# Half-size products for ten units of a convolution's input and 21 of the last FFN, with the weight sums on VectorE and on GpSimd

## The reference, cut to what matters

```python
def short_conv_mixer(h, w_in, conv_w, w_out):          # first mixer of the first block
    b_gate, c_gate, u = jnp.split(h @ w_in, 3, axis=-1)
    v = c_gate * u
    conv = ...                                          # causal, 3 taps per channel
    return (b_gate * conv) @ w_out

def conv_ffn(h, w_up, conv_w, conv_b, w_down, grid):    # last FFN of the second block
    gate, up = jnp.split(h @ w_up, 2, axis=-1)
    gate = dwconv_grid(gate, conv_w, conv_b, grid)      # 3x3 taps per channel, grid 4 x 64
    return (jax.nn.gelu(gate, approximate=True) * up) @ w_down
```

## Time and profile before

| what | value |
|---|---|
| median of 3 runs | 3435.51 us (3429.36 to 3435.82) |
| the profiled execution | 3436.1 us |
| its span, first to last instruction | 3434.3 us |
| instructions in the span | 54420 |
| PE busy | 3189.5 us, 93% of the span |
| DVE busy | 995.1 us, 29% |
| ACT busy | 593.8 us, 17% |
| POOL busy | 225.3 us, 7% |
| mean granted clock of TensorE | 0.943 of 2.4 GHz |

### The profile page before, as it was taken

One profiled execution on the slowest core, in us unless ns is written; L12 is line 12 of the kernel. 1 busy time (PEld: TensorE's weight loads), 2 busy tenths in 40 slices (PEclk: granted clock), 3 DMA queues, 4 the chain that ended last, 5 costly groups with the idle time before them and its releaser, 6 DMA issues. The chain is left out here.

```text
span 3434.3 us, 54420 instructions
## 1 busy us (share of the span) xinstructions
PE 3189.5 (93%) x24210; PEld 1926.6 (56%) x24210; DVE 995.1 (29%) x2185; ACT 593.8 (17%) x1336; POOL 225.3 (7%) x198
## 2 busy tenths in 40 slices
PE   7999996899999999989988999999898888888998
PEld 4788784633323332254765544444544777777887
DVE  0255115311100110023064233420313555461560
ACT  1010012210000000032144200000202343432100
POOL 0000000000000000000032100000000223131000
PEclk9999998899999999979989899999798989998999
DMA  9778841169988889922002133333211000004340
GB/s 365 280 281 326 326 176 65 56 265 377 377 352 344 341 360 376 390 77 74 2 1 98 49 123 146 119 127 121 80 50 58 14 21 17 14 3 180 120 155 13
DMA packets 88492, 577.04 MB, mean 168 GB/s; under 512 B 9536, under 2 KB 15936, under 8 KB 20672
## 3 DMA queue, kind: packets, MB, share of 16 engines
q1 hardware_dynamic: 84800, 568.27, 42.4%
q10 hardware_dynamic: 3456, 5.24, 0.4%
HBM read 567.19 MB, written 6.29 MB: 167 GB/s over the span
## 5 line engine op out<-in xcount | busy, mean ns | idle before, releaser
L267 PE MATMUL ps<-H,ring 128*128 128x256 f32 (+1 forms) x2928 | 909.4, 473 | 19.3 <-ACT H L557 8.9
L267 PEld LDWEIGHTS ps<-H,ring 128*128 128x128 f32 x2928 | 567.4, 195 | 361.1 <-issue 309.5
L267 PE MATMUL ps<-W,ring 128*128 128x256 f32 (+1 forms) x1488 | 470.3, 477 | 11.3 <-DVE W L2858 8.0
L1706 PE MATMUL ps<-ring,W 128*32 128x512 f32 (+1 forms) x2816 | 474.1, 596 | 1.7 <-ACT H L1766 1.7
L267 PEld LDWEIGHTS ps<-W,ring 128*128 128x128 f32 x1488 | 284.6, 193 | 199.2 <-issue 172.3
L1706 PEld LDWEIGHTS ps<-ring,W 128*32 128x32 f32 (+1 forms) x2816 | 136.6, 123 | 288.1 <-issue 285.5
L1730 PE MATMUL ps<-ring,W 128*64 128x512 f32 (+1 forms) x1408 | 240.1, 598 | 0.0
L1988 DVE SCALAR_TENSOR_TENSOR W<-ps,vec,W 128x189 f32<-128x189 f32 (+3 forms) x396 | 173.3, 438 | 14.0
L1730 PEld LDWEIGHTS ps<-ring,W 128*64 128x64 f32 (+1 forms) x1408 | 65.0, 123 | 169.3 <-issue 169.3
L3383 POOL TENSOR_TENSOR ring<-ring 128x512 f32<-128x512 f32 x96 | 124.5, 1315 | 529.7 <-DVE ring L3407 461.8
L1814 DVE TENSOR_TENSOR H<-ps,H 128x256 f32<-128x256 f32 x66 | 28.0, 424 | 358.0 <-ACT H L1757 358.0
(11 more groups left out here) (427 smaller groups left out, 3130.0 us busy)
## 6 DMA issues: line engine op xcount, KB each, us to landing
ring<-weights SPq DMA_DIRECT2D x528, 1024.0 KB, 7.1
rkv<-W ACTq DMA_DIRECT2D x16, 256.0 KB, 2.0
ring<-rkv SPq DMA_DIRECT2D x8, 512.0 KB, 3.7
X<-tokens SPq DMA_DIRECT2D x2, 1024.0 KB, 8.6
ring<-rw_tiles SPq DMA_DIRECT2D x8, 256.0 KB, 2.7
rkv<-W ACTq DMA_DIRECT2D x8, 128.0 KB, 2.1
ring<-rkv SPq DMA_DIRECT2D x8, 128.0 KB, 3.7
out<-X SPq DMA_DIRECT2D x8, 128.0 KB, 1.9
```

Source lines behind the costliest of these rows:

```text
L267: mm = pe.matmul(out(o), lhsT=k.ring[:, k.slot(at), p * P:(p + 1) * P], rhs=rhs(kk), start=kk == 0, stop=kk == kt - 1)
L1706: mm = pe.matmul(ps[at:at + n, r, :], lhsT=moe.Hg[:, kt, FIRST * e + first:FIRST * e + first + n], rhs=w[e][:, kk * WIDE:(kk + 1) * WIDE], ...
```

## The change

Three things change.

1. `stage_conv_in`: the weights are reordered (`CONV_ORDER`) so that a unit holds the u output and the c_gate output of one group, and the last four units the b_gate outputs. Unit 0 and unit 11 stay with `gemm`; units 1 to 10 go through `Seven`, with the weight sums on DVE. The convolution of group u-1 is made at the beginning of unit u, the product with b_gate at once after each unit, into `tmp` in place, and the last two straight out of PSUM. PE's first product of a unit waits for ACT's copies of the unit before.
2. `stage_out_residual` takes its input as an argument: `tmp` here, `k.H` at its other call.
3. `stage_last_ffn` takes the place of `stage_conv_ffn` for layer 1: unit 0 with `gemm`, units 1 to 21 through `Seven`, where `seven.made = k.pool` puts the four sums on GpSimd. The gate and the up output of such a unit are put together in SBUF (`firsts`, `seconds`), and the taps and the last product read them there. DVE's order in unit u: five taps of f = u-1, early, four taps, the product of f = u-2, late.

Core of the diff (the index tables and what repeats are left out):

```diff
@@ stage_conv_in
+CONV_ORDER = [o for i in range(8) for o in (16 + i, 8 + i)] + list(range(8))
-    p = Plan([i // KD for i in range(n_out * KD)], ada.units)
+    p = Plan([i // KD for i in range(n_out * KD)], ada.units, seven=units - 1)
...
+            for u in range(1, units - 1):
+                seven.products(pe, u, first_free, sums_done)
+                for place, v in p.beside(u):
+                    ada.unit(pe, place, v)
...
+            for u in range(1, units - 1):
+                convolve(u - 1) if u <= 8 else gated(u - 1)
+                seven.early(dve, u)
+                if u + 2 < units:
+                    seven.sums(dve, u + 1)
+                seven.late(dve, u)
+            gated(units - 2)
+            for o in range(2):
+                dve.wait_ge(k.mm.sem, k.mm.at(out_done[n_out - 2 + o]))
+                link.mark(dve.tensor_tensor(tmp[:, 6 + o, :], tmp[:, 6 + o, :], k.ps[:, 4 + o, 0:S], ALU.mult))
@@ class Seven
+    def sums(self, eng, u):
+        eng.wait_ge(k.w_in[k.slot(place)], k.landed(place))
         if u >= 3:
+            self.product_done(eng, u - 2, self.P3)
+        eng.tensor_tensor(S[:, 0, :], A(2, 1), A(2, 2), ALU.add).then_inc(made.sem, 1)
+        eng.tensor_tensor(S[:, 2, :], A(1, 1), A(2, 1), ALU.subtract).then_inc(made.sem, 1)
+        eng.wait_ge(made.sem, made.at(done["S1", u]))
+        eng.tensor_tensor(S[:, 1, :], S[:, 0, :], A(1, 1), ALU.subtract).then_inc(made.sem, 1)
+        eng.wait_ge(made.sem, made.at(done["S2", u]))
+        eng.tensor_tensor(S[:, 3, :], A(1, 2), S[:, 1, :], ALU.subtract).then_inc(made.sem, 1)
@@ stage_last_ffn
+    seven = Seven(k, p, k.H[:, :, cols], n, KF * n, done)
+    seven.made = k.pool
+    firsts = [k.W[:, at:at + n] for at in (14080, 14848)]
+    seconds = seven.up + [k.W[:, 15104:15360]]
+    seven.top = lambda u: firsts[u % 2][:, h:n]
+    seven.bottom = lambda u: seconds[u % 3]
...
+                y, x = conv[:, f % 2, 0:n], firsts[f % 2] if f else k.ps[:, 6, 0:n]
...
+                link(dve.tensor_scalar(y, x, w(1, 1), k.v("fcb", layer * KF + f), ALU.mult, ALU.add))
+                yield
...
+                    ins = dve.scalar_tensor_tensor(yo, xg[:, r0 + a:r1 + a, c0 + b:c1 + b], w(a + 1, b + 1), yo, ALU.mult, ALU.add)
...
+            def gated(f):
...
+                dve.tensor_tensor(A[:, f, :], seven.bottom(f) if f else k.ps[:, 7, 0:n], conv[:, f % 2, 0:n],
+                                  ALU.mult).then_inc(k.dve.sem, 1)
...
+            seven.tokens(dve)
+            for u in range(1, KF):
+                convolution = taps(u - 1)
+                for _ in range(5):
+                    next(convolution)
+                seven.early(dve, u)
+                for _ in convolution:
+                    pass
+                if u > 1:
+                    gated(u - 2)
+                seven.late(dve, u)
+            gated(KF - 2)
+            for _ in taps(KF - 1):
+                pass
+            gated(KF - 1)
...
+        def _(pool):
+            pre.pool(pool)
+            pre.ready(pool, KD - 1)
+            for u in range(1, KF):
+                seven.sums(pool, u)
+            rms.add(pool)
...
+            for u in range(1, KF):
+                seven.copy_first(act, u)
+                seven.product_done(act, u, seven.P2)
+                if u > 2:
+                    act.wait_ge(k.dve.sem, k.dve.at(done["conv", u - 2]))
+                act.activation(firsts[u % 2][:, 0:h], seven.bank(seven.FIRST), ACT.Copy).then_inc(k.act.sem, 1)
+                gelu(u - 1)
```

More of the change, by code:

```diff
@@ L755, in _ @@
             pre.scalar(act)
-            for o in range(n_out):
+            for o in range(2):
                 act.wait_ge(k.mm.sem, k.mm.at(out_done[o]))
-                act.activation(Z[:, o, :], k.ps[:, o % 4, 0:S], ACT.Copy).then_inc(k.act.sem, 1)
+                act.activation(Z[:, CONV_ORDER[o], :], k.ps[:, o, 0:S], ACT.Copy).then_inc(k.act.sem, 1)
+            for u in range(1, units - 1):
+                seven.copy_first(act, u)
+                seven.product_done(act, u, seven.P2)
+                act.activation(Z[:, CONV_ORDER[2 * u], 0:h], seven.bank(seven.FIRST), ACT.Copy).then_inc(k.act.sem, 1)
         @block.vector
@@ L762, in _, with outputs, convolve @@
             pre.vector(dve)
+            seven.sums(dve, 1)
+            for kk in range(KD):
+                pre.ready(dve, kk)
+            seven.tokens(dve)
             link = Link(k.dvel, dve)
-            for i in range(8):
-                dve.wait_ge(k.act.sem, k.act.at(17 + i))
+            def outputs(u):
+                dve.wait_ge(k.act.sem, k.act.at(done["first", u]))
+                dve.wait_ge(k.dve.sem, k.dve.at(done["C12", u]))
+            def convolve(i):
+                outputs(i)
                 v, y = Z[:, 16 + i, :], tmp[:, i, :]
@@ L771, in _, with gated, stage_out_residual @@
                 link(dve.scalar_tensor_tensor(y[:, 2:S], v[:, 0:S - 2], w(0), y[:, 2:S], ALU.mult, ALU.add))
-            dve.wait_ge(k.mm.sem, k.mm.at(out_done[n_out - 1]))
-            for i in range(8):
-                link.mark(dve.tensor_tensor(k.H[:, i, LAT], tmp[:, i, :], Z[:, i, :], ALU.mult))
+            def gated(u):
+                outputs(u)
+                for i in (2 * u - 16, 2 * u - 15):
+                    link.mark(dve.tensor_tensor(tmp[:, i, :], tmp[:, i, :], Z[:, i, :], ALU.mult))
+            for u in range(1, units - 1):
+                convolve(u - 1) if u <= 8 else gated(u - 1)
[4 more added lines that the diff above has]
+            gated(units - 2)
+            for o in range(2):
+                dve.wait_ge(k.mm.sem, k.mm.at(out_done[n_out - 2 + o]))
+                link.mark(dve.tensor_tensor(tmp[:, 6 + o, :], tmp[:, 6 + o, :], k.ps[:, 4 + o, 0:S], ALU.mult))
             link.close()
     k.mm.base += total
-    k.act.base += n_out
+    k.act.base += done["first", units - 2]
+    k.dve.base += n
     k.dma.base += 32
     k.unit += len(p.order)
-def stage_out_residual(k, gate, rms, finish=None):
+    return tmp
+def stage_out_residual(k, x, gate, rms, finish=None):
     nc = k.nc
@@ L3615, in layout @@
     first = wide_units(i["mod_w"][0, 0])
[L3616 removed]
+    parts = [first[0:8], woven(units(tiles(i["conv_w_in"][0])[CONV_ORDER]), wide_units(i["mod_w"][0, 1]), first[8:12]), units(tiles(i["conv_w_out"][0])),
              woven(swiglu_units(i["ffn_w_gate"][0], i["ffn_w_up"][0], i["ffn_w_down"][0]),
```

161 lines of the change are left out of this document (137 added, 24 removed).

## The result

The changed kernel takes 3478.9 us (median of 4 runs, 3475.85 to 3480.8), the kernel before beside it 3432.88 (4 runs, 3429.36 to 3435.82): a ratio of 1.0136 [1.0122, 1.015], slower by 46 us. The forecast was 3479, 43.4 us over the profiled execution before, in a range of 3450 to 3508.

The account below looks back on a forecast made before the run. TensorE, busy 93% of the span, was taken to bound the kernel, with VectorE becoming the last FFN's limit. First stage -11.3 and FFN +54.7 gave +43.4 us, so 3479 us; range 3450 to 3508.

Parts of the forecast that it names:

- Convolution's input, -11.3: First changed stage: units of 6.26 us for 6.91, shorter end wait, no clock drop; -11.3 us, bounds -8.4 and -11.3.
- Unit of the last FFN, 5.9 + 3.1 = 9.0 us: VectorE's 5.9 us plus three meetings with GpSimd make it the limit; 9.0 us per unit, bounds 8.0 and 10.0.
- Clock within the units, +8: Last FFN: TensorE's idling drops its clock in many units, costing 0.4 us a unit; +8 us, bounds 0 and 36.
- Tail, +4.3: End of the last FFN's units: TensorE waits 6.3 us for VectorE and gelu instead of 1.99; +4.3 us.
- Clock behind it, +1.2: Down projection: the longer wait before it costs more full-speed time, 2.9 us lost instead of 1.7; +1.2 us.
- The start, 0: Start of the last FFN: token sums meet GpSimd's sums, some 4 us, hidden behind TensorE's unit 0; costs nothing.
- the -0.65 that I had for unit 1: Last FFN: the first unit in seven products has little beside it and saves TensorE 0.65 us.
- undisturbed: Rival: VectorE and GpSimd do not disturb each other, VectorE stays under TensorE in the last FFN; 3416 us, chance 0.09.
- Few meetings: Rival: one to two meetings per unit of the last FFN, 7.0 to 8.0 us each; 3431 to 3451 us, chance 0.07.
- full lock: Rival: shared port locked for the full instruction, 9.6 us per last-FFN unit; 3491 us, chance 0.2 with four meetings included.
- stuck clock: Rival: TensorE stays at 1.2 GHz in the last FFN, 12.5 us per unit; 3541 us, chance 0.06.
- the first stage did give its part: Answers a rival: convolution's input gains nothing because VectorE's 5.8 us exceed 6.26; 11 us more, 3490 us, chance 0.05.

Follow-up runs that it names:

- Experiment 1: The changed kernel with the last FFN as before, so only the convolution's input in seven products: 3421.56 us, ratio 0.9962 against the kernel before.
- experiment 6: The changed kernel with the first stage's weight sums on GpSimd as well: 3482.37 us, ratio 1.0149 against the kernel before.
- experiment 5: The changed kernel with nine unread matmuls added before P4 of every unit, filling TensorE's idle time: 3468.3 us, ratio 1.0106 against the kernel before.
- experiment 2: The changed kernel with gate and up output put together in spare PSUM banks, GpSimd keeping its sums: 3413.76 us, ratio 0.9945 against the kernel before.
- experiment 4: The changed kernel with GpSimd making weight sums for units 1 and 2 only, taps staying in SBUF: 3413.76 us in one run.
- experiment 8: The changed kernel with each GpSimd sum of 128x512 split into two of 128x256: 3449.81 us, ratio 1.0061 against the kernel before.

## Why the forecast held, step by step

**Convolution's input, -11.3: -11.2 measured.** The unit of 6.26 is 6.25; VectorE's 5.8 us in it stayed covered; the wait at the end is 0.87 (I took 1.09), and the clock behind it did not fall, as I had taken from its distance to 3.65. The DMA share came out at 0.91, as estimated. Experiment 1 shows that this part stands by itself, and experiment 6 how near it was: the same stage with its sums on GpSimd gives half of the gain back.

**Unit of the last FFN, 5.9 + 3.1 = 9.0 us: 8.86 measured.** The standing still is 2.94 us per unit on average: (0.953 - 0.413) in the scale and 8 x (0.732 - 0.432) in the taps. The average takes in the last two scales and their taps, which met nothing. In the steady units of 8.87 us of experiment 5 three taps lose 2.66 us together and the scale 0.37, so the work without meetings is 8.87 - 3.03 = 5.8. I had counted three meetings at 1.03. The count was too low and the price too high, and these errors cancel: that the term came out within 0.14 us is in part luck. I had given one GpSimd operation to the time in which VectorE reads PSUM; in fact it starts beside VectorE's last late operation and catches part of the scale behind it. The row that I priced from, L3462, lost 1.03 us a time; a tap of nearly the same shape lost 1370 - 485 = 0.89 in experiment 6, as the taps do here. L3462 started 0.03 us behind GpSimd, the taps of experiment 6 0.22 to 0.24, and both ended 0.28 us behind it: the dearer one had more of GpSimd's operation before it. And that the price follows GpSimd's duration, could not show, since all operations of GpSimd there are of one size.

The Trainium skill, "SBUF — State Buffer", section "SBUF: two separate sides", has the two engines' shared port pair held exclusively for a full instruction. The runs agree that one side stands still (experiments 2 and 4 remove it from either end), and that it does so to the end of GpSimd's instruction, since no caught operation ended before it. That an operation with an input in PSUM does not take part is measured here as well. The 9.6 us were too much all the same, against 8.86: what lies before VectorE's start and the last 0.15 to 0.28 us of a caught operation are not added to GpSimd's time, which is also why two halves cost less than one whole.

**Clock within the units, +8: +13.3 to +14.8 measured** (experiment 5). This is the term that was mis-sized. I expected falls "in many units" and charged 0.4 us each, since most of the slow time should lie where TensorE waits anyway. The trace shows 12 long distances in 20, and each costs 0.9 to 1.6 us over 8.87, up to near the bound of 1.7: the slow stretch begins at most 0.4 us before P4, or within it (2.08 us for its eight records in the timeline above), so that P4 and P3 run slow with C12 waiting for them, and hardly any of it falls into the idle time. The twelve falls came behind waits of 1.89 to 2.35 us. Of the seven units of 8.86, three had a shorter wait (1.61 to 1.76 us) and four one of 2.34 or 2.35. Why these four were not followed by a fall stays open; no run here tells it.

**Tail, +4.3: +3.8** (5.79 against 1.99). **Clock behind it, +1.2: +1.0.** Both by their own steps, and experiments 2 and 4 have the same wait (5.90 and 5.78 us) without a meeting.

**The start, 0: +1.1, by another cause.** I had costed the meetings of the token sums with GpSimd's first sums at nothing, because TensorE is busy with unit 0. The timeline after:

```profile
3178.72 1.26 POOL L967 TENSOR_TENSOR W<-ring 128x512 f32<-128x512 f32 x1 [10.44 <-ACT H L557]
3178.77 1.75 DVE L953 TENSOR_TENSOR W<-H 128x512 f32<-128x512 f32 x1 [1.80 <-ACT H L557]
3179.93 1.71 POOL L968 TENSOR_TENSOR W<-ring 128x512 f32<-128x512 f32 x1
```

The two engines take turns here, 1.7 us for each operation on either side, where a 128x512 sum takes VectorE 0.69 and GpSimd 1.27 undisturbed. Yet TensorE doesn't wait once from its first matmul in the stage to the end of unit 1, so in this trace the meetings cost nothing, as forecast. Of the 56.2 us, 51.9 + 3.8 are the units and the tail; the remaining +0.5 stands against the -0.65 that I had for unit 1. This 1.1 us is the clock of unit 0, whose matmuls are the same in both programs. The first 10 us of the stage before and after (windows):

```profile
3187.55:3197.55 10.00, 8.79 (x32) 7.49 (x33) 5.75 (x16) 5.32 (x9) 0.00 (x0) 0.74 0.01 2
3174.14:3184.14 10.00, 8.80 (x27) 7.28 (x28) 8.16 (x13) 4.04 (x8) 5.35 (x4) 0.63 0.00 0
```

TensorE is busy equally long, but at a mean clock of 0.63 instead of 0.74, and unit 0 takes it 10.0 us instead of 8.9. The full clock came back later, and no run varies what sets that moment. In experiment 2, with the same meetings and a clock of 0.77 in these 10 us, TensorE reached unit 1 earlier and did wait 0.60 us for the last token sum.

Altogether the sum came out 0.1 us from the median. That is closer than the working deserves, and luck: the difference of the medians is 46.0 us against 43.4, and the parts were less exact. The units without the clock came to 37.1 to 38.5 instead of 41.8, the clock to 5 to 7 more than I gave it, and the stretch that did not change happened to be 2 us shorter. The rivals: *undisturbed* is what experiments 2 and 4 made of the kernel, 3413.8 us against the 3416 of its working, so the saving was there, and the meetings alone took it away and more. *Few meetings*, *full lock* as I priced it (9.6 us) and *stuck clock* are each excluded by the distances (8.86, and back to full clock within the unit), and the first stage did give its part.

## What to carry to other kernels

Before work is moved from VectorE to GpSimd, look at what VectorE does at that time and where it reads. Operations with all inputs in SBUF stood still until GpSimd's operation was over (0.89 us beside one of 1.27), so four sums that would have cost VectorE 2.75 us cost it 2.94; operations with one input in PSUM lost nothing, and the remedy was to leave the data in PSUM (two lines of addresses and one more wait, 65 us). A wait that this puts before matmuls costs more than its length if the clock falls behind it: here 13 to 15 us on top of 37 to 39.

Where two engines exclude each other, price it from both: duration and number of the operations on the side that disturbs and how far they are when the other side starts, not only the longest duration on the side that is disturbed.

## What the runs showed of the hardware beyond expectation

- A caught operation of VectorE of 256 columns or fewer ended 0.15 to 0.28 us behind GpSimd's, never before it. The price of a meeting is what is left of GpSimd's instruction at the start: for the taps 0.89 us beside one of 1.27 us and 0.34 beside one of 0.72, so smaller pieces cost less in sum (1.97 instead of 2.94 us per unit) though there are twice as many.
- A scale with one SBUF tile as its only tensor input is caught as well (353 to 1242 ns), and 128x512 operations of both engines slow each other down to about 1.7 us each; with short operations on VectorE's side, GpSimd lost little (1.26 to 1.46 us).
- With one input in PSUM nothing was caught in 141 taps that ran beside GpSimd's sums (experiment 2), though they wrote to SBUF and had their second input there.
- The clock fell behind TensorE idle times of 1.89 to 2.35 us in twelve units of the changed kernel, and did not in seven others, four of which had the same 2.34 or 2.35 us and the same work around them. Behind the 1.38 us of the steady units of experiment 8 and the 0.87 of the first stage it did not.
